# Attention of block 1 with transposed scores, and an earlier start of its output product

## The chip, the cores and the metric

One core of one Trainium2 chip runs the whole program in one launch. The metric is the device time in microseconds (us), median of the runs shown. The engines are called by what they do: TensorE (PE in the profile) multiplies matrices, PEld is its load of the stationary side; VectorE is DVE, ScalarE is ACT, GpSimd is POOL, SyncE is SP, from which most DMAs are issued.

## The reference

512 tokens of width 1024 pass twice through block 1 (a mixer of attention and a two-way state-space scan, then a feed-forward part) and once through block 2. The change is in block 1's mixer alone:

```python
    def one_block(qi):
        s = jnp.einsum("bqgrd,bkgd->bgrqk", qi, k)
        p = jax.nn.softmax(s, axis=-1)
        return jnp.einsum("bgrqk,bkgd->bqgrd", p, v)
...
        attn_out = blocked_gqa(q, k, v).astype(x.dtype)
        ssd_out = ssd_mixer(z, xbc_raw, dt_raw, conv_w[i], conv_b[i], dt_bias[i], a_log[i],
                            d_skip[i], ssd_norm_w[i])
        mixed = jnp.concatenate([attn_out, ssd_out], axis=-1)
        x = x + jnp.einsum("ble,ed->bld", mixed, w_out[i])
```

There are 8 query heads of 64 and 2 key/value heads, over 512 tokens; the state-space part has 8 heads, 4 chunks of 128 tokens and both directions.

## The kernel before

All data are fp32. Large products are made of three fp32r products of split operands: each factor is held as a high part (rounded to fp32r) and a low part (the rest), and high x high, high x low and low x high are summed in PSUM. One such product of a 128 x 128 weight tile with 512 tokens is a "row": the three passes of lines 1469 to 1471. The weights are streamed from HBM in slots, and each slot is split by ScalarE (high, L1805) and VectorE (low, L2216). Small products are in plain fp32, which the trace shows as two passes for each product; a transpose is one pass.

The instructions of every engine stand in one fixed order. The class Order writes it down beforehand by playing the program through with a table of costs (TIMES, in us) and a few delays (DELAY). Each chain of work (attention, conv, ssd_decay, ssd_rows, ...) is a generator that adds its steps when their inputs are due by that clock and when PSUM banks are free (room, take, free). Every engine then runs its part of that order strictly in sequence, with semaphores where data cross. There are eight PSUM banks; while the input projection runs, three serve its rows and five ("side") all the rest; afterwards all eight serve both.

Block 1 of layer l: the wide product gives z, v and dt with tokens on partitions; thirteen column tiles follow (k, four of q, eight of x, B and C for the convolution). After each q or k tile come its norm, rotation and split (rsq, rmm, rroot, rcs, rope, qhi, qlo; SP swaps halves by DMA into ROT). Then come attention and the state-space part, then the output product.

Attention before, for each pair of heads and block of 128 queries (16 such steps, pair_chunk, and two head_chunk each):

- qk (L1686, L1687): scores with queries on partitions and 512 keys along the row, from the high and low keys; each head's high and low queries lie in the two halves of 128 partitions.
- max, exp with the sum as a second output, nrm (reciprocal), prs (scaling), on VectorE and ScalarE (L2494, L2000, L2499, L2006).
- pT (L1428): four 128 x 128 transposes for each head, and pta (L2013), their copy.
- pv (L1701): eight products for the two heads, in two column halves of the array.
- yv (L2018 on ScalarE, L2504 on VectorE): the split of 128 tokens of output into YHI and YLO.

State space, for each chunk c of four: dec (L1645, products of 32 rows in four row groups, into four banks), dexp (ScalarE), mask, w and xc (VectorE), off and yt (PE), goff, ytc, yb (transposes), gyb, gsq and zout (L2479); after the last chunk four transposes of Z (zT, L1428) and yz. The output product of layer l is split: the first four output tiles are made as one group, row after row, r = 0 to 3 being attention's and 4 to 7 the state-space part's; the other four follow. It begins when all outputs of attention and the last yb have been put into the order:

```python
        self.run(lambda: ("yv", l, NH // 2 * CH - 1) in self.n and ("yb", l, CH - 1) in self.n)
```

X waits in HBM meanwhile and is brought back by GpSimd's DMAs after the last yz.

## Time and profile before

| what | value |
|---|---|
| median of 3 runs | 2699.52 us (2699.2 to 2699.63) |
| the profiled execution: span | 2697.8 us, 1.7 us under the median; the rest lies before and after its first and last instruction |
| TensorE, VectorE, ScalarE busy in the span | 99%, 57%, 43% |
| granted TensorE clock | 0.999 of 2.4 GHz |
| block 1, layer 0: projection ends, output product begins | 127.6 us, 206.3 us |
| layer 1: the same | 734.2 us, 812.8 us |

A row of the profile gives busy time or a start and a duration. TensorE's durations include the time in which a pass drains, which overlaps the next one; what a pass costs in a flow is the distance between starts. Times are from the start of the span.

### The profile page before, as it was taken

The page shows a single profiled execution, that of the slowest core. Times are in us where ns is not written, and L with a number is a line of the kernel's source. Part 1 is how long each engine was busy: PE and PEld are TensorE (multiplying, and loading weights), DVE is VectorE, ACT ScalarE, POOL GpSimd, SP SyncE. Part 2 cuts the span into 40 slices and gives each one's busy share as a digit, 9 for nine tenths or more (in the row PEclk, how much of TensorE's full clock was granted, in tenths as well). Part 3 has the DMA queues.
Part 4 walks back from the last instruction along what each step waited for, and adds up shares of the span by engine and source line. Part 5 has one row for each costly group of instructions (what it writes and reads, how often), then busy time and mean ns, then how long its engine had stood idle before and what let it go on. Part 6 is the DMA issues. An engine that isn't in the chain of part 4 may idle for free.

```text
span 2697.8 us, 33846 instructions
## 1 busy us (share of the span) xinstructions
PE 2665.9 (99%) x13860; PEld 2195.1 (81%) x13860; DVE 1526.9 (57%) x2142; ACT 1173.5 (43%) x1732; POOL 26.8 (1%) x45
## 2 busy tenths in 40 slices
PE   9989999999989999999999999999999999999998
PEld 8777888888777888888888888888777888888887
DVE  7885444345885444344444356899978844544433
ACT  6784332225784322233322234455688452432221
POOL 0000000000000000000000000000000000000000
PEclk9999999999999999999999999999999999999999
DMA  6303333324303333333333342222223432333332
GB/s 216 94 2 110 100 96 95 98 83 148 94 2 110 102 94 97 97 94 97 100 94 96 98 138 86 72 74 76 77 86 96 133 94 94 98 98 94 98 94 67
DMA packets 75801, 255.55 MB, mean 95 GB/s; under 512 B 9088, under 2 KB 12288, under 8 KB 75264
## 3 DMA queue, kind: packets, MB, share of 16 engines
q1 hardware_dynamic: 73136, 240.29, 29.3%
q0 software_dynamic: 2512, 13.11, 1.3%
q8 instruction: 110, 1.80, 0.3%
q14 instruction: 43, 0.35, 0.0%
HBM read 241.30 MB, written 8.39 MB: 93 GB/s over the span
## 4 chain that ended last, share of the span: by engine, by line
PE 93%; DVE 4%; ACT 3%; issue 1%; DVEq 0%; ACTq 0%
PE PS L1469 27%; PE PS L1471 27%; PE PS L1470 27%; PE PS L1719 1%; PE PS L1701 1%; PE PS L1428 1%; PE PS L1488 1%; PE PS L1487 1%; PE PS L1489 1%; DVE WLO L2216 0%; PE PS L1665 0%; ACT WHI L1805 0%; PE PS L1537 0%; PE PS L1535 0%; PE PS L1539 0%
## 5 line engine op out<-in xcount | busy, mean ns | idle before, releaser
L1469 PE MATMUL PS<-HHI,WHI 128*128 128x512 f32 x2256 | 893.2, 396 | 0.0
L1471 PE MATMUL PS<-HHI,WLO 128*128 128x512 f32 x2256 | 878.8, 390 | 0.0
L1470 PE MATMUL PS<-HLO,WHI 128*128 128x512 f32 x2256 | 878.3, 389 | 0.0
L2216 DVE TENSOR_TENSOR WLO<-WR,WHI 128x1024 fp32r<-128x1024 f32 (+2 forms) x450 | 535.0, 1191 | 495.4 <-ACT WHI L1805 492.2
L1805 ACT CAST WHI<-WR 128x1024 fp32r<-128x1024 f32 (+2 forms) x450 | 457.5, 1018 | 445.6 <-PE PS L1471 421.9
L1469 PEld LDWEIGHTS PS<-HHI,WHI 128*128 128x128 f32 x2256 | 423.6, 188 | 92.1 <-issue 4.8
L1470 PEld LDWEIGHTS PS<-HLO,WHI 128*128 128x128 f32 x2256 | 423.7, 188 | 89.9 <-issue 4.1
L1471 PEld LDWEIGHTS PS<-HHI,WLO 128*128 128x128 f32 x2256 | 423.4, 188 | 88.8
L1469 PE MATMUL PS<-FHI,WHI 128*128 128x512 f32 x682 | 265.3, 389 | 0.0
L1470 PE MATMUL PS<-FLO,WHI 128*128 128x512 f32 x682 | 265.3, 389 | 0.0
L1471 PE MATMUL PS<-FHI,WLO 128*128 128x512 f32 x682 | 265.3, 389 | 0.0
L1877 ACT CAST FHI<-SQF 128x512 fp32r<-128x512 f32 x88 | 54.5, 620 | 330.3 <-DVE SQF L2285 330.3
L1873 ACT ACTIVATE SQF<-SQF 128x512 f32<-128x512 f32 x88 | 55.6, 632 | 307.4 <-DVE SQF L2278 307.3
L2606 DVE SCALAR_TENSOR_TENSOR CVA<-CU,VEC,CVA 128x511 f32<-128x511 f32 (+14 forms) x240 | 162.9, 730 | 1.8 <-ACT CVA L2110 1.8
L2285 DVE TENSOR_TENSOR SQF<-SQF,PS 128x512 f32<-128x512 f32 x88 | 60.6, 688 | 166.0 <-PE PS L1471 162.1
L1469 PEld LDWEIGHTS PS<-FHI,WHI 128*128 128x128 f32 x682 | 128.0, 188 | 26.8
L1470 PEld LDWEIGHTS PS<-FLO,WHI 128*128 128x128 f32 x682 | 128.0, 188 | 26.5
L1471 PEld LDWEIGHTS PS<-FHI,WLO 128*128 128x128 f32 x682 | 128.0, 188 | 26.4
L2278 DVE TENSOR_TENSOR SQF<-PS,RS 128x512 f32<-128x512 f32 x88 | 60.8, 691 | 142.2 <-PE PS L1471 140.9
L1469 PE MATMUL PS<-YHI,WHI 128*128 128x512 f32 x320 | 128.1, 400 | 2.2 <-DVE WLO L2216 2.1
L1471 PE MATMUL PS<-YHI,WLO 128*128 128x512 f32 x320 | 124.7, 390 | 0.0
L1470 PE MATMUL PS<-YLO,WHI 128*128 128x512 f32 x320 | 124.6, 389 | 0.0
(381 smaller groups left out, 2727.5 us busy)
## 6 DMA issues: line engine op xcount, KB each, us to landing
WR<-in_stream SPq DMA_DIRECT2D x402, 512.0 KB, 3.6
WR<-in_stream SPq DMA_DIRECT2D x32, 384.0 KB, 3.0
xkeep<-X POOLq DMA_DIRECT2D x3, 2048.0 KB, 9.4
X<-xkeep POOLq DMA_DIRECT2D x24, 256.0 KB, 4.7
WR<-in_stream SPq DMA_DIRECT2D x16, 328.0 KB, 4.0
ROT<-RQ SPq DMA_DIRECT2D x40, 64.0 KB, 2.0
X<-in_xin SPq DMA_DIRECT2D x8, 256.0 KB, 4.9
out<-X SPq DMA_DIRECT2D x8, 256.0 KB, 2.2
```

What stands on the lines that cost most here:

```text
L1428: t = e.transpose(out[:, i * P:(i + 1) * P], src, ident)
L1469: e.matmul(out, hi[:, i, :], xhi, start=first, stop=False)
L1470: e.matmul(out, hi[:, i, :], xlo, start=False, stop=False)
L1471: t = e.matmul(out, lo[:, i, :], xhi, start=False, stop=final)
L1487: e.matmul(out, xhi, hi[:, i, :], start=r == 0, stop=False)
L1805: e.copy(hi, raw).then_inc(S["act_high"], 1)
L1873: e.activation(SQ[:, j % 2, :], SQ[:, j % 2, :], ACT.Silu).then_inc(S["act_silu"], 1)
L1877: e.copy(FHI[:, j, :], HF[:, j % 2, :]).then_inc(S["act_xhigh"], 1)
L2216: e.tensor_tensor(lo, raw, hi.bitcast(F32), ALU.subtract).then_inc(S["dve_low"], 1)
L2278: e.tensor_tensor(SQ[:, j % 2, :], PS[o.bank["gate", f, j]][:, :], RS[:, :], ALU.mult).then_inc(S["dve_gs"], 1)
L2285: e.tensor_tensor(HF[:, j % 2, :], SQ[:, j % 2, :], PS[o.bank["up", f, j]][:, :], ALU.mult).then_inc(S["dve_mul"], 1)
L2606: e.scalar_tensor_tensor(acc[:, s:T], CU[:, j, 0:T - s], vec("cvw", 8 * (TAPS - 1 - s) + j), acc[:, s:T], ALU.mult, ALU.add).then_inc(S["d ...
```

## The change

The scores are computed twice. First qk makes them as before with queries on partitions, but from high parts alone, with 64 rows for each of two heads, and only for the maximum of each query (over tokens c, c + 4, c + 8, ... for each c of four). The negated maxima of a head (NM) go by DMA (mrow) as one row under a copy of the head's high queries (qdup, also a DMA) in QM. Then ks makes the scores with keys on partitions: the high keys times the queries' high and low parts, plus the low keys and a row of ones times QM, so that the maximum is already subtracted. exp of that needs no sum and no scaling, and its result is the stationary side of pv, which moves V with a column of ones (65 columns) and gives for each head tokens on partitions with the sum in column 64. yn divides by it; after two heads hT transposes four 128 x 128 blocks and yv splits 512 tokens at once. Exponentials lie in five buffers, and in nine after the 24th tile. The transposes of probabilities, their copies, the scaling and the accumulated sums are gone. GpSimd sets the ones by two memsets. The delays pace1 and pace2 become 0.1. The output product's group is put into the order once yt of chunk 2 is, and each attention row needs only its own pair of heads. The core of the diff (the semaphore names, group names and times of removed steps are left out, and in the functions of the class Order the removed lines too):

```diff
-    "qk": (("pe", 0.92),), "qhi": (("act", 0.76785),), "qlo": (("dve", 1.3),), "pT": (("pe", 0.45),), "pv": (("pe", 0.95),),
+    "qk": (("pe", 0.25),), "ks": (("pe", 0.46),), "mrow": (("sp", 0.3),), "qdup": (("sp", 0.1),), "qhi": (("act", 0.76785),), "qlo": (("dve", 1.3),), "hT": (("pe", 0.45),), "pv": (("pe", 1.9),),
...
-DELAY = {"v": 0.38043, "zsilu": 0.77358, "pace1": 0.37491, "pace2": 6.0781, "turned": 0.81963, "sums": 0.30369, "ss": 1.401,
-         "hsum": 0.075925, "picked": 0.55886, "lru": 5.6906, "sq": 0.27228, "third": 0.17664, "merged": 0.20081, "until": 0.087442}
+DELAY = {"v": 0.38043, "zsilu": 0.77358, "pace1": 0.1, "pace2": 0.1, "turned": 0.81963, "sums": 0.30369, "ss": 1.401,
+         "hsum": 0.075925, "picked": 0.55886, "lru": 5.6906, "sq": 0.27228, "third": 0.17664, "merged": 0.20081, "until": 0.087442, "row": 2.6}
...
-PR_OF = [i % 3 if i < 8 else (3, 4, 2, 0, 1)[(i - 8) % 5] for i in range(4 * NH)]
-PR_BEFORE = {i: max(k for k in range(i) if PR_OF[k] == PR_OF[i]) for i in range(4 * NH) if PR_OF[i] in PR_OF[:i]}
+TILES = NH * CH
+EARLY = 24
+PT_OF = [i % 5 if i < EARLY else (4, 5, 6, 7, 8, 0, 1, 2)[i - EARLY] for i in range(TILES)]
+PT_BEFORE = {i: max(k for k in range(i) if PT_OF[k] == PT_OF[i]) for i in range(TILES) if PT_OF[i] in PT_OF[:i]}
...
+    def maxima(self, l, m):
+        for c in range(CH):
+            yield from self.room(2)
+            while self.tokens_wait:
+                yield 0.1
+            for h in (2 * m, 2 * m + 1):
+                self.take(("qk", l, h, c), "side")
+            yield self.add("qk", l, m, c)
+            for h in (2 * m, 2 * m + 1):
+                last = self.add("max", l, h, c)
+                self.free(("qk", l, h, c), ("dve_max", last))
+            yield self.pace
+        yield last
+        for h in (2 * m, 2 * m + 1):
+            self.spawn(self.head(l, h))
+    def head(self, l, h):
+        if h > 0:
+            yield from self.added(("ks", l, h - 1, CH - 1))
+        if h >= 2:
+            yield from self.until(("ks", l, h - 2, CH - 1))
+        self.add("qdup", l, h)
+        self.add("mrow", l, h)
+        yield DELAY["row"]
+        for k in range(CH):
+            i = CH * h + k
+            if i in PT_BEFORE:
+                yield from self.added(("pv", l, PT_BEFORE[i] // CH))
+            if PT_OF[i] >= 5:
+                yield from self.added(("qlo", l, 4))
+            yield from self.room()
+            while self.tokens_wait:
+                yield 0.1
+            self.take(("ks", l, h, k), "side")
+            yield self.add("ks", l, h, k)
+            exp = self.add("exp", l, i)
+            self.free(("ks", l, h, k), ("act_exp", exp))
+            yield self.pace
         yield exp
+        if h > 0:
+            yield from self.added(("yn", l, h - 1))
         yield from self.room()
+        self.take(("pv", l, h), "side")
+        yield self.add("pv", l, h)
+        done = self.add("yn", l, h)
+        self.free(("pv", l, h), ("dve_yn", done))
+        if h % 2:
+            yield done
+            yield from self.room()
+            self.take(("hT", l, h // 2), "side")
+            yield self.add("hT", l, h // 2)
+            self.free(("hT", l, h // 2), ("dve_yv", self.add("yv", l, h // 2)))
 
     def attention(self, l):
         yield from self.until(("v", l))
+        for m in range(NH // 2):
+            yield from self.until(("kdup", l), ("qlo", l, 1 + m))
+            if m > 0:
+                yield from self.added(("qk", l, m - 1, CH - 1))
+            self.spawn(self.maxima(l, m))
 
...
-        self.run(lambda: ("yv", l, NH // 2 * CH - 1) in self.n and ("yb", l, CH - 1) in self.n)
+        self.run(lambda: ("yt", l, 2) in self.n)
         self.advance(SPL)
         self.product_group(("mixed", l), [(("out", 2 * l, j), "w_out", l, j * P) for j in range(CH)],
-                           {DT - 4 + i: ("yz", l, i) for i in range(4)})
+                           {i: ("yv", l, i) if i < 4 else ("yz", l, i - 4) for i in range(DT)})
...
-    V = sb("V", 192, [CH, P])
-    PR = sb("PR", 194, [2, T])
-    PT = sb("PT", 198, [2, 2, CH, P])
-    NM = sb("NM", 206, [8])
-    RSM = sb("RSM", 206.0625, [8])
-    RIN = sb("RIN", 206.125, [8])
+    V = sb("V", 192, [CH, 2, 65])
+    PT = sb("PT", 194.03125, [5, T])
+    QM = (sb("QM", 76, [T], F32R), sb("QM2", 204.03125, [T], F32R))
+    NM = sb("NM", 206.03125, [NH, CH], F32R)
+    RIN = sb("RIN", 206.1875, [2, CH])
+    YVS = (sb("YV", 180, [4, T]), sb("YV2", 207.5, [4, T]))
...
-                        q.wait_ge(S["dve_yv"], n["yv", of[0], CH * r + CH - 1])
+                        q.wait_ge(S["dve_yv"], n["yv", of[0], r])
...
             elif kind == "qk":
-                l, u = a
-                m, c = u // CH, u % CH
-                q.wait_ge(s_keys, 64 * (l + 1))
+                l, m, c = a
+                q.wait_ge(s_keys, 48 * (l + 1))
                 q.wait_ge(S["dve_qlow"], n["qlo", l, 1 + m])
-                for i in range(2):
-                    emptied(q, ("qk", l, 2 * u + i))
-                    out, left = PS[o.bank["qk", l, 2 * u + i]][:, :], query(2 * m + i)[:, c * P:(c + 1) * P]
-                    e.matmul(out, left, KDS[0][:, m // 2, :], start=True, stop=False)
-                    t = e.matmul(out, left, KDS[1][:, m // 2, :], start=False, stop=True)
+                for i, half in enumerate((slice(0, 64), slice(64, P))):
+                    emptied(q, ("qk", l, 2 * m + i, c))
+                    t = e.matmul(PS[o.bank["qk", l, 2 * m + i, c]][:, :], query(2 * m + i)[half, c::CH],
+                                 KDS[0][half, m // 2, :], start=True, stop=True)
                 t.then_inc(S["pe_qk"], 1)
-            elif kind == "pT":
-                l, i = a
-                q.wait_ge(S["act_prs"], n["prs", l, i])
-                transposes(step, [PRS[PR_OF[i]][:, k * P:(k + 1) * P] for k in range(CH)]).then_inc(S["pe_turn"], 1)
+            elif kind == "ks":
+                l, h, k = a
+                emptied(q, step)
+                q.wait_ge(S["pool_ones"], 2 * l + 2)
+                q.wait_ge(s_qm[h % 2], 32 * (4 * l + h // 2 + 1))
+                keys = slice(k * P, (k + 1) * P)
+                e.matmul(PS[o.bank[step]][:, :], KDS[0][:, h // 4, keys], query(h), start=True, stop=False)
+                e.matmul(PS[o.bank[step]][:, :], KDS[1][0:65, h // 4, keys], QM[h % 2][0:65, :], start=False, stop=True
+                         ).then_inc(S["pe_ks"], 1)
             elif kind == "pv":
-                l, u = a
-                m = u // CH
+                l, h = a
+                out = PS[o.bank[step]]
                 emptied(q, step)
+                q.wait_ge(S["pool_ones"], 2 * l + 1)
                 q.wait_ge(S["act_v"], n["v", l])
-                q.wait_ge(S["act_pt"], n["pta", l, 2 * u + 1])
-                for k in range(CH):
-                    for i in range(2):
-                        t = e.matmul(PS[o.bank[step]][64 * i:64 * i + 64, 0:P], V[:, k, 64 * (m // 2):64 * (m // 2) + 64],
-                                     PT[:, u % 2, i, k, :], start=k == 0, stop=k == CH - 1)
+                q.wait_ge(S["act_exp"], n["exp", l, CH * h + CH - 1])
+                for c in range(CH):
+                    for k in range(CH):
+                        t = e.matmul(out[:, 65 * c:65 * c + 65], PTS[PT_OF[CH * h + k]][:, c * P:(c + 1) * P], V[:, k, h // 4, :],
+                                     start=k == 0, stop=k == CH - 1)
                 t.then_inc(S["pe_pv"], 1)
+            elif kind == "hT":
+                l, m = a
+                emptied(q, step)
+                q.wait_ge(S["dve_yn"], n["yn", l, 2 * m + 1])
+                transposes(step, [heads_tokens(m)[:, c, :] for c in range(CH)]).then_inc(S["pe_turn"], 1)
...
             elif kind == "exp":
                 l, i = a
-                k = i % 8
-                q.wait_ge(S["dve_max"], n["max", l, i])
-                if i in PR_BEFORE:
-                    q.wait_ge(S["pe_turn"], n["pT", l, PR_BEFORE[i]])
-                elif i >= 8:
-                    q.wait_ge(S["dve_qlow"], n["qlo", l, 2])
-                e.activation(PRS[PR_OF[i]], PS[o.bank["qk", l, i]][:, :], ACT.Exp, bias=NM[:, k:k + 1],
-                             accum_out=RSM[:, k:k + 1]).then_inc(S["act_exp"], 1)
-            elif kind == "prs":
-                l, i = a
-                k = i % 8
-                q.wait_ge(S["dve_nrm"], n["nrm", l, i // 2])
-                e.activation(PRS[PR_OF[i]], PRS[PR_OF[i]], ACT.Copy, scale=RIN[:, k:k + 1]).then_inc(S["act_prs"], 1)
-            elif kind == "pta":
-                l, i = a
-                u = i // 2
-                q.wait_ge(S["pe_turn"], n["pT", l, i])
-                if u >= 2:
-                    q.wait_ge(S["pe_pv"], n["pv", l, u - 2])
-                e.copy(PT[:, u % 2, i % 2, :, :].rearrange("p k q -> p (k q)"), PS[o.bank["pT", l, i]][:, :]).then_inc(S["act_pt"], 1)
+                q.wait_ge(S["pe_ks"], n["ks", l, i // CH, i % CH])
+                if PT_OF[i] >= 5:
+                    q.wait_ge(S["dve_qlow"], n["qlo", l, 4])
+                if i in PT_BEFORE:
+                    q.wait_ge(S["pe_pv"], n["pv", l, PT_BEFORE[i] // CH])
+                e.activation(PTS[PT_OF[i]], PS[o.bank["ks", l, i // CH, i % CH]][:, :], ACT.Exp).then_inc(S["act_exp"], 1)
             elif kind == "yv":
-                l, u = a
-                at_ = slice(u % CH * P, (u % CH + 1) * P)
-                q.wait_ge(S["pe_pv"], n["pv", l, u])
-                e.copy(YHI[:, u // CH, at_], PS[o.bank["pv", l, u]][:, 0:P]).then_inc(S["act_yv"], 1)
+                l, m = a
+                q.wait_ge(S["pe_turn"], n["hT", l, m])
+                e.copy(YHI[:, m, :], PS[o.bank["hT", l, m]][:, :]).then_inc(S["act_yv"], 1)
...
             elif kind == "max":
-                l, i = a
-                k = i % 8
-                q.wait_ge(S["pe_qk"], n["qk", l, i // 2])
-                if i >= 8:
-                    q.wait_ge(S["act_exp"], n["exp", l, i - 8])
-                e.tensor_reduce(NM[:, k:k + 1], PS[o.bank["qk", l, i]][:, :], AX, ALU.max, negate=True).then_inc(S["dve_max"], 1)
-            elif kind == "nrm":
-                l, u = a
-                k = 2 * u % 8
-                q.wait_ge(S["act_exp"], n["exp", l, 2 * u + 1])
-                e.reciprocal(RIN[:, k:k + 2], RSM[:, k:k + 2]).then_inc(S["dve_nrm"], 1)
+                l, h, c = a
+                q.wait_ge(S["pe_qk"], n["qk", l, h // 2, c])
+                e.tensor_reduce(NM[:, h, c:c + 1], PS[o.bank["qk", l, h, c]][:, :], AX, ALU.max, negate=True).then_inc(S["dve_max"], 1)
+            elif kind == "yn":
+                l, h = a
+                got = PS[o.bank["pv", l, h]][:, 0:65 * CH].rearrange("p (c x) -> p c x", c=CH)
+                q.wait_ge(S["pe_pv"], n["pv", l, h])
+                settle(e.reciprocal(RIN[:, h % 2, :], got[:, :, 64]))
+                e.tensor_tensor(heads_tokens(h // 2)[:, :, 64 * (h % 2):64 * (h % 2) + 64], got[:, :, 0:64],
+                                RIN[:, h % 2, :].unsqueeze(2).to_broadcast([P, CH, 64]), ALU.mult).then_inc(S["dve_yn"], 1)
             elif kind == "yv":
-                l, u = a
-                at_ = slice(u % CH * P, (u % CH + 1) * P)
-                q.wait_ge(S["act_yv"], n["yv", l, u])
-                e.tensor_tensor(YLO[:, u // CH, at_], PS[o.bank["pv", l, u]][:, 0:P], YHI[:, u // CH, at_].bitcast(F32),
+                l, m = a
+                q.wait_ge(S["act_yv"], n["yv", l, m])
+                e.tensor_tensor(YLO[:, m, :], PS[o.bank["hT", l, m]][:, :], YHI[:, m, :].bitcast(F32),
                                 ALU.subtract).then_inc(S["dve_yv"], 1)
...
+            elif kind == "v":
+                l, = a
+                done(q, ("z", l))
+                e.memset(V[:, :, :, 64:65], 1.0).then_inc(S["pool_ones"], 1)
+            elif kind == "kdup":
+                l, = a
+                q.wait_ge(s_keys, 48 * (l + 1))
+                q.wait_ge(S["pool_ones"], 2 * l + 1)
+                e.memset(KDS[1][64:65, :, :].bitcast(F32), 1.0).then_inc(S["pool_ones"], 1)
...
+            elif kind == "qdup":
+                l, h = a
+                rows = slice(0, 64) if h % 2 == 0 else slice(64, P)
+                q.wait_ge(S["act_qhigh"], n["qhi", l, 1 + h // 2])
+                if h >= 2:
+                    q.wait_ge(S["pe_ks"], n["ks", l, h - 2, CH - 1])
+                elif l > 0:
+                    q.wait_ge(S["dve_xlow"], n["hlo", 2 * l, DT - 1])
+                e.dma_start(QM[h % 2][0:64, :].bitcast(F32), query(h)[rows, :].bitcast(F32)).then_inc(s_qm[h % 2], 16)
+            elif kind == "mrow":
+                l, h = a
+                q.wait_ge(S["dve_max"], n["max", l, h, CH - 1])
+                e.dma_start(QM[h % 2][64:65, :].bitcast(F32), NM[:, h, :].bitcast(F32)).then_inc(s_qm[h % 2], 16)
             elif kind == "vectors":
```

## Rows read from the trace of the kernel before

**Rows 1.** The page, busy time of each engine over the span.
```profile
PE 2665.9 (99%) x13860; PEld 2195.1 (81%) x13860; DVE 1526.9 (57%) x2142; ACT 1173.5 (43%) x1732; POOL 26.8 (1%) x45
```
**Rows 2.** Windows: length, busy PE, PEld, DVE, ACT, POOL (instructions), clock, DMA, GB/s.
```profile
80.00:127.60 47.60, 47.56 (x245) 37.73 (x244) 37.15 (x57) 36.67 (x66) 0.54 (x1) 1.00 0.31 97
127.60:206.30 78.70, 69.66 (x838) 56.40 (x836) 66.79 (x132) 69.11 (x163) 4.66 (x4) 1.00 0.01 2
206.30:220.00 13.70, 13.05 (x66) 10.55 (x65) 6.36 (x10) 5.03 (x11) 2.12 (x4) 1.00 0.20 51
734.20:812.80 78.60, 69.58 (x836) 56.33 (x835) 66.75 (x132) 69.02 (x163) 4.66 (x4) 1.00 0.01 2
```
**Rows 3.** Timeline of PE, 118 to 124 us: start, duration, instruction.
```profile
119.36 0.40 PE L1471 MATMUL PS<-HHI,WLO 128*128 128x512 f32 x1
119.80 0.63 PE L1428 MATMUL PS<-CON,PR 128*128 128x128 f32 x4
120.18 0.47 PE L1469 MATMUL PS<-HHI,WHI 128*128 128x512 f32 x1
120.49 0.39 PE L1470 MATMUL PS<-HLO,WHI 128*128 128x512 f32 x1
120.72 0.40 PE L1471 MATMUL PS<-HHI,WLO 128*128 128x512 f32 x1
```
**Rows 4.** Waits, 127.6 to 206.3 us: who for whom, total, times, longest.
```profile
DVE YLO L2504 <- ACT YHI L2018: 7.8, 5, 3.6
...
PE PS L1428 <- DVE YLO L2504: 1.9, 2, 1.7
...
PE PS L1428 <- ACT PR L2000: 1.4, 1, 1.4
...
PE PS L1624 <- ACT PR L2000: 0.6, 1, 0.6
...
PE PS L1428 <- ACT PT L2013: 0.5, 1, 0.5
```
**Rows 5.** Timeline of PE, 151.45 to 157.9 us.
```profile
152.53 1.97 PE L1701 MATMUL PS<-PT,V 128*64 128x128 f32 x32
154.42 1.17 PE L1645 MATMUL PS<-RUNB,RUNA 32*128 32x128 f32 x32
155.53 0.50 PE L1686 MATMUL PS<-KDH,QS 128*128 128x512 f32 x1
```
**Rows 6.** PE's groups, 127.6 to 206.3 us: busy us, mean ns, idle before.
```profile
L1701 PE MATMUL PS<-PT,V 128*64 128x128 f32 x224 | 14.6, 276 | 1.2 <-DVE RUNB L2432 0.8 <-ACT PT L2013 0.4
```
**Rows 7.** Timeline of PE, 55.25 to 56.9 us: the cumulative sums.
```profile
55.53 1.22 PE L1607 MATMUL PS<-SD,CON 128*128 128x64 f32 x10
56.56 0.48 PE L1469 MATMUL PS<-HHI,WHI 128*128 128x512 f32 x1
```
**Rows 8.** ScalarE's groups, 127.6 to 206.3 us.
```profile
L2013 ACT COPY PT<-PS 128x512 f32<-128x512 f32 x28 | 15.5, 608 | 0.8 <-PE PS L1428 0.6
...
L2006 ACT ACTIVATE PR<-PR,RIN 128x512 f32<-128x512 f32 x11 | 7.7, 751 | 0.0
```
**Rows 9.** VectorE's groups, 127.6 to 206.3 us.
```profile
L2494 DVE TENSOR_REDUCE NM<-PS 128x1 f32<-128x512 f32 x24 | 15.4, 683 | 1.6 <-PE PS L1687 1.6
...
L2504 DVE TENSOR_TENSOR YLO<-PS,YHI 128x128 fp32r<-128x128 f32 x14 | 4.0, 287 | 8.0 <-ACT YHI L2018 7.8
...
L2499 DVE RECIPROCAL RIN<-RSM 128x2 f32<-128x2 f32 x13 | 1.9, 156 | 0.0
...
L2442 DVE TENSOR_TENSOR MF<-PS,CON 128x256 f32<-128x256 f32 x4 | 1.7, 417 | 0.0
```
**Rows 10.** DMA issues: out, engine, count, KB each, median us to landing.
```profile
ROT<-RQ SPq DMA_DIRECT2D x40, 64.0 KB, 2.0
...
KDH<-KDH SPq DMA_DIRECT2D x4, 128.0 KB, 4.3
```
**Rows 11.** Timeline, 209 to 236 us: VectorE's last scaling and the first transpose.
```profile
209.50 0.61 DVE L2479 TENSOR_SCALAR Z<-YA,SS 128x256 f32<-128x256 f32 x2 [0.40 <-ACT SS L1788]
...
212.09 0.60 PE L1428 MATMUL PS<-CON,Z 128*128 128x128 f32 x4
```

77 lines of the change are left out of this document (17 added, 60 removed).

## The prediction

> **What bounds the kernel now.** I began with the page's busy shares: TensorE is in use for 99% of the span [rows 1]. A busy row of TensorE includes its drain, so this says that little is idle, not that nothing can be saved. Next came the windows view, cut where block 1 changes character [rows 2]. While the input projection runs (80 to 127.6 us) TensorE is busy to within 0.04 us. From the projection's last product (127.6) to the first of the output product (206.3) there is a stretch of 78.7 us with attention and the state-space part alone. There TensorE is busy 69.66 us, ScalarE 69.11, VectorE 66.79: three engines, each close to full and each waiting for the others. The second layer has the same stretch from 734.2, of 78.6 us. The reader is to see that only these two stretches hold idle time, 9.0 us each by this view. Outside them TensorE has none, so that each product added there is paid in full, and attention that is moved ahead of 127.6 only changes sides.
>
> More than 9.0 us is slack, since drains hide in busy. The timeline shows the edges [rows 3]: starts of rows follow each other in about 0.23 us, but with four transposes between them, 119.36 to 120.49 holds two rows and the burst: 1.13 us, less 0.46 is 0.67, where four transposes in steady flow take 0.44 (priced below). So a burst of plain fp32 that stands alone costs 0.23 us of edges besides its work. The waits of the stretch [rows 4] name who is late: TensorE waits 4.4 us for scaled probabilities, copies of transposes and exponentials on ScalarE, or for VectorE at YLO; VectorE itself stood 7.8 us behind ScalarE's copy of an attention output. ScalarE's queue is the place where attention and state space get into each other's way.
>
> **Products of one layer.** Scores before: 16 steps of four 512-wide fp32r passes; passes of this width stand 0.23 apart [rows 3]: 64 x 0.231 = 14.8 us. After: the transposed scores (ks) are 32 steps of two such passes, again 14.8; the maxima's pass (qk) is 16 steps of two products of 64 rows each, in the two halves of the array. The only row-tiled products here are the decay's, 32 rows high: 32 passes in 155.53 - 154.42 = 1.11 us [rows 5], 0.035 each, where a full pass takes 0.11 (below). So row tiles run side by side; I take 0.25 for a pair, 4.0 us, and 0.46 (one after the other), 7.4, as the other end. The decay's burst has an edge of its own: eight groups of four at 0.11 are 0.88, and it took 1.11. Sixteen such edges would be 3.7 us; I put 1 against what is given back below.
>
> The Trainium skill ("TensorEngine Tiling (Array Packing)", section Key Properties) has every change of the tiling mode drain TensorE. That speaks against many single pairs among full products; at the decay's edge, by estimate, it would make the sum 2.7 us a layer worse than mine.
>
> Transposes before: 32 x 4 = 128; after: 16. The burst of four in [rows 3] gives 0.095 (0.38 / 4, its end hidden by the next product) to 0.117 (0.63, less 0.28 for one, over three steps); at 0.109 each this is -112 x 0.109 = -12.2 us.
>
> Output of attention (pv) before: 16 steps of 16 passes in column halves; two steps took 154.42 - 152.53 = 1.89 us [rows 5], so 0.95 a step and 15.2 us. After: 8 steps of 16 products, fp32, thus two passes each, with probabilities of 128 x 128 as the stationary side and 65 columns moving. The nearest row is the cumulative sum: a 128 x 128 stationary side, 64 columns moving, ten passes in 1.22 us by the row, less the 0.27 to 0.28 that one fp32 pass lasts [rows 6], over nine steps: 0.105; from its start to the next product 1.03, 0.103 [rows 7]. I take 0.11, as these passes are no faster than transposes that move 128 columns: the stationary side sets the pace. 8 x 32 x 0.11 = 28.2 us, +13.0. The lower bound is the pace of the old column halves, 1.89 / 32 = 0.059: 15.1 us, so 0.
>
> The Trainium skill ("TensorE: Matmul & The Clock Gate", section LDWEIGHTS) has the load of a stationary side take its columns over 1.2 GHz whatever the rows, 107 ns for 128; the trace agrees with 0.103 to 0.105. The same page's isolated gap ("Back-to-back issue gap") would make a 65-column pass about 30 ns, a step of 32 under 1 us and the layer's pv 7.6 us, an estimate that the row of the cumulative sum speaks against.
>
> Sum on TensorE: +4.0 - 12.2 + 13.0 = **+4.8 us a layer**, +8.2 with the pairs in series.
>
> **The other engines, a layer.** ScalarE loses 32 rescalings of 0.75 and 32 copies of 0.61 [rows 8] (in steady flow some 0.1 less each), its 32 reads of the accumulator and twelve of sixteen output copies: about 40 us of work, some 33 of it in the stretch, where it was 69 of 78.7. VectorE keeps 32 maxima of 0.68; the small outputs (16 of 0.29) and reciprocals give way to 8 divisions over 256 columns, priced at 0.42 as the mask of that width out of PSUM plus a reciprocal, and 4 outputs of 512, 0.69: 4.6 + 2.4 out, 4.6 + 2.8 in [rows 9]. That is nothing, but VectorE keeps its 67 us in the stretch, and 206.3 can come no nearer than that to 127.6.
>
> Five tiles hold a head's exponentials until the seventh head, so three of four exponentials wait for the pv of the head before; that pv stands ahead of their scores in TensorE's order, so this adds nothing by itself, but it lets no head run ahead of its neighbour.
>
> New on SP's queue: eight copies of the query's high half and eight rows of maxima. The SBUF copies of before land 2.0 us (64 KB) to 4.3 us (128 KB) after issue [rows 10]. TensorE has 49.2 / 8 = 6.2 us of work a head and there are two buffers, so I cost them at nothing; without that cover (the first head, and any whose maxima are late) it is 2 to 4.3 us each. In the projection these DMAs wait between the weight loads, and a load behind them has the 5.5 us that 24 rows give it. On GpSimd two small memsets stand before the limits' DMA: nothing, as its queue is empty. VectorE's division waits for the whole pv of 3.5 us, with maxima and state-space work queued behind; that is the wait that takes YLO's place.
>
> **What is given back, a layer.** (1) Of the 4.4 us of TensorE's waits in [rows 4] I count 3.5 as gone: the instructions at fault are removed or ScalarE is half empty. (2) Edges: 48 fp32 bursts of attention become 12, at most 36 x 0.23 = 8.3 us less. Many stand beside other fp32 work and share edges, and 14 of the 16 old pv are in the stretch [rows 6], so I take 4, less the 1 of the pairs: 3. (3) The output product starts with the attention rows of four tiles, 48 passes or 11 us, while the last chunks run; before, it began at 206.3, when VectorE's last scaling stood at 209.50 and the first transpose of it at 212.09 [rows 11]. The moved passes are no less work; what they fill is idle time, 0.65 us of the third window of [rows 2] and, as an estimate, 1.9 of the 9.0 of the second, at its end: 2.5. Sum 9.0. Against +4.8: **-4.2 a layer, -8.4 in all**. The profiled execution's span is 2697.8 us; its time is 1.7 less than the median 2699.5, so the median becomes about **2691**. Both ends for the range: everything given back (9.0 + 0.65 + 8.3 = 18.0) is -13.2 a layer, 2673; nothing, and pairs in series, +8.2, 2716.
>
> **Rivals.** *The added passes win* (slower). Place: the stretch. If the divisions behind pv and the maxima behind the score banks bring back as much waiting as ScalarE's relief removes, only the sum of products is left: +4.8 x 2 = +9.6, 2709, with pairs in series 2716. For it: VectorE has 67 us in the stretch, and the order's cost table calls pv 1.9 where I get 3.5, so eight times 1.6 us are scheduled as if free. Against it: TensorE is then the one that is never idle. It decides from less than 4.8 us a layer given back. Chance 0.23.
>
> *Even.* The output product holds four of the eight banks, and the last chunk's decay wants four at once; it then comes after all attention, the 2.5 us of (3) are lost, and one or two late rows of maxima take another 2: -4.2 + 4.5, 2700, range 2695 to 2704. Chance 0.17.
>
> *Most is given back.* With ScalarE out of the way the order packs TensorE nearly full: 14 us instead of 9.0, -9.2 a layer, 2681. The same time would come if the 65-column passes were at the lower bound (13.0 less a layer would even give 2665); of this end a tenth of this case. Chance 0.13.
>
> My forecast has 0.47, its own range 2685 to 2695.
>
> **How the numbers follow.** Under 2694.1 (0.2%, about what a measurement of this kernel can tell from no change) lie the whole of the third rival and nearly all of the forecast, 0.44: faster 0.57. Within it: 0.17 and 0.03: same 0.20. Slower 0.23. The range runs from 2676 to 2710: below it lies half of the third rival's tail, above it the pairs in series.
>
> **What the profile would show.** The pv line with 512 passes in two layers, 3.4 to 3.6 us a step of 32, and qk's two passes starting within some ns; if they are 0.23 apart, the maxima cost double. Between the projection's last product and the last transpose of the state-space output, ScalarE down from 69 to about 35 to 40 us busy, VectorE still at 65 to 70, TensorE's idle time under 5 us. Rows of the output product between the last two chunks. Wrong I would be if ks waited for SP's DMAs in most heads, if VectorE stood for whole pv steps while a decay burst waited for its banks, or if the old idle time of 9.0 us was there under new names.

## The result and the profile after

The change made the kernel slower: median 2724.51 us (2721.7 to 2727.13, 4 runs) against 2699.47, ratio 1.0091, 95% interval [1.0077, 1.0105]. I had forecast 2691 with a range up to 2710 and given "slower" 0.23. The profiled execution's span is 2722.9 us, 25.1 above that of before. Where the first layer's mixer is done (the sum of the next norm) is at 264.52 us before and 274.94 after, in layer 1 at 871.09 and 894.48: +10.4 and another +13.0, so all but 1.7 us of the loss is where the change is. The last 1.7 us are the spell of half clock at 2084 us that comes up below, in block 2, where both kernels do the same work. Of the experiments' executions, two stand at a far lower granted clock (11248.86 us at 0.226 with the wide pv, 4646.68 us at 0.623 with GpSimd's queue and full maxima) and are in no comparison.

The page after, and the windows view (columns as in [rows 2]), cut at the projection's end, the first output row, and the same in layer 1:

```profile
PE 2690.1 (99%) x13700; PEld 2216.7 (81%) x13700; DVE 1530.4 (56%) x2118; ACT 1086.4 (40%) x1512; POOL 27.8 (1%) x49
```
```profile
80.00:143.30 63.30, 58.81 (x284) 46.29 (x282) 47.17 (x71) 27.72 (x45) 0.54 (x1) 0.97 0.27 74
143.30:204.10 60.80, 58.59 (x631) 49.38 (x630) 50.56 (x91) 30.01 (x60) 3.09 (x3) 0.97 0.06 13
204.10:232.00 27.90, 24.64 (x160) 20.24 (x159) 12.83 (x24) 8.16 (x22) 1.04 (x1) 1.00 0.06 20
700.00:763.00 63.00, 58.11 (x277) 45.79 (x275) 45.55 (x70) 26.66 (x44) 0.59 (x2) 0.95 0.26 74
```

Against [rows 2] two things are new. The stretch without projection and output rows shrank from 78.7 us with 9.0 idle to 60.8 with 2.2 idle, as hoped; but the projection, in which TensorE had not been idle at all, now ends 15.7 us later (part of that is attention moved ahead) and holds 4.5 us of idle time. And the granted clock, 1.00 in every window of before, is 0.97 in the projection and in the stretch of layer 0, and 0.95 in the projection of layer 1.

The timeline at the idle time, SP's queue and TensorE together (start, duration; SPq is the issue of a DMA):

```profile
103.02 0.51 SPq L2765 DMA_DIRECT2D ROT<-RQ  x1
103.57 0.59 SPq L2766 DMA_DIRECT2D ROT<-RQ  x1
104.20 0.59 SPq L2765 DMA_DIRECT2D ROT<-RQ  x1
104.27 0.39 PE L1485 MATMUL PS<-HHI,WLO 128*128 128x512 f32 x1
104.83 0.59 SPq L2766 DMA_DIRECT2D ROT<-RQ  x1
105.47 0.59 SPq L2781 DMA_DIRECT2D QM<-QS  x1
106.11 0.59 SPq L2785 DMA_DIRECT2D QM<-NM  x1
108.28 0.77 PE L1707 MATMUL PS<-QS,KDH 128*128 128x512 f32 x1 [3.63 <-DMA QM<-NM]
```
VectorE in the same trace, its last maxima for the first two heads:
```profile
93.82 1.29 DVE L2500 TENSOR_REDUCE NM<-PS 128x1 fp32r<-128x512 f32 x2 [0.85 <-PE PS L1698]
```

The maxima were done at 95.1, and their row was issued at 106.11, 11.0 us later. It stood on SP behind the copies of the next query tile (ROT<-RQ), which had to wait for ScalarE to evict that tile. TensorE is then idle for 3.63 us (4.01 between starts, where a pass takes 0.23). The second head's row costs 0.87 us of idle time, about 1.2 between starts beyond the pass; in layer 1 it is 4.04 and 0.84. These four are all the waits of ks for its DMAs: in each layer the other six heads don't wait.

TensorE's rows for the new products:

```profile
131.18 0.39 PE L1707 MATMUL PS<-QS,KDH 128*128 128x512 f32 x1
131.41 0.40 PE L1708 MATMUL PS<-QM,KDL 65*128 65x512 f32 x1
131.74 0.63 PE L1698 MATMUL PS<-KDH,QS 64*128 64x512 f32 x2
132.30 0.50 PE L1483 MATMUL PS<-HHI,WHI 128*128 128x512 f32 x1
132.63 0.40 PE L1484 MATMUL PS<-HLO,WHI 128*128 128x512 f32 x1
...
136.87 3.68 PE L1719 MATMUL PS<-V,PT 128*128 128x65 f32 x32
140.49 0.62 PE L1698 MATMUL PS<-KDH,QS 64*128 64x512 f32 x2
```

ks is 0.23 a pass; pv is 140.49 - 136.87 = 3.62 us for 32 passes, 0.11 each. The maxima's pair (its two passes start 3 to 4 ns apart in 30 of the trace's 32 pairs, at most 9, so they run side by side) takes 0.56 us from its start to the next row's, and the full passes ahead of it and behind it take 0.33 instead of 0.23: 0.76 us in all for 0.23 of work, 0.53 of edges. Behind a pv burst, which has its own edge, the pair adds less.

The granted clock in its spells, by windows cut to them:

```profile
107.90:111.30 3.40, 3.02 (x7) 2.47 (x8) 3.07 (x7) 1.71 (x3) 0.00 (x0) 0.50 0.25 49
148.80:152.20 3.40, 3.40 (x49) 2.24 (x51) 3.40 (x7) 0.56 (x1) 0.00 (x0) 0.51 0.21 40
725.70:732.50 6.80, 6.22 (x13) 4.29 (x14) 4.90 (x9) 2.31 (x4) 0.00 (x0) 0.50 0.25 77
```

0.50 is 1.2 of 2.4 GHz. The clock of the first and third falls in or behind the idle 3.63 and 4.04 us, that of the second behind 1.98 us in which TensorE waits for VectorE's convolution (2.6 between starts). With two more (766.6, 3.4 us; 2084.2, 3.4 us) these are 20.4 us at half speed. TensorE is idle for 1.1 of them, so some 9.7 us are lost, an estimate. Before has no such spell until its last 4.2 us.

A gap of this size does not always bring a spell. The last of the five stands behind a gap in block 2 that before has too, and there the clock stays:

```profile
2060.46 1.12 PE L1766 MATMUL PS<-XB,GW 128*128 128x512 f32 x2 [1.89 <-DVE XB L2613]
```
```profile
2055.00:2075.00 20.00, 18.11 (x76) 14.01 (x75) 18.15 (x24) 17.96 (x22) 0.00 (x0) 1.00 0.37 112
```
and in the trace after:
```profile
2083.84 1.76 PE L1789 MATMUL PS<-XB,GW 128*128 128x512 f32 x2 [1.87 <-DVE XB L2620]
```
```profile
2084.20:2087.60 3.40, 3.40 (x6) 1.42 (x5) 3.33 (x5) 3.37 (x4) 0.00 (x0) 0.50 0.47 137
```

So spells come and go between executions, and a difference between two kernels has to be freed of them. The table takes from each profiled execution's span half of the time at half clock in which TensorE was not idle (the last microseconds of the program left out). The last column is thus an estimate of the span at full clock.

| kernel | span, us | half clock, us | span at full clock, estimate |
|---|---|---|---|
| before | 2697.8 | 0 | 2697.8 |
| changed | 2722.9 | 20.4 | 2713.2 |
| early start alone | 2713.5 | 13.6 | 2707.7 |
| early start after the last decay | 2700.5 | 0 | 2700.5 |
| late start | 2719.9 | 17.1 | 2711.6 |
| full maxima | 2717.5 | 13.6 | 2711.6 |
| each pair twice | 2726.1 | 13.7 | 2720.2 |
| scores due later | 2737.1 | 68.3 | 2703.4 |
| GpSimd's queue | 2708.9 | 10.2 | 2703.9 |
| wide pv | 2731.8 | 30.7 | 2717.5 |
| wide pv, full maxima, late start | 2711.7 | 13.6 | 2705.0 |
| full maxima, late start, price altered | 2719.9 | 27.3 | 2708.6 |
| the same on GpSimd's queue | 2718.6 | 20.5 | 2709.5 |
| no maxima | 2697.6 | 10.2 | 2692.5 |
| GpSimd's queue, full maxima | 2705.7 | 10.2 | 2700.8 |
| GpSimd's queue, full maxima, late start | 2701.2 | 6.8 | 2698.0 |

### The profile page after: what moved, and what is told of

It reads as the page before. It is cut to its first block, busy times and chain, and to the rows that moved or that the text cites. A ratio compares the mean times of both kernels' runs of the same rounds, so it can differ in the third digit from the quotient of the medians.

```text
span 2722.9 us, 33265 instructions
## 1 busy us (share of the span) xinstructions
PE 2690.1 (99%) x13700; PEld 2216.7 (81%) x13700; DVE 1530.4 (56%) x2118; ACT 1086.4 (40%) x1512; POOL 27.8 (1%) x49
## 4 chain that ended last, share of the span: by engine, by line
PE 93%; DVE 4%; ACT 2%; issue 1%; SPq 0%; DMA 0%; DVEq 0%; ACTq 0%
PE PS L1483 27%; PE PS L1485 27%; PE PS L1484 27%; PE PS L1719 2%; PE PS L1742 1%; PE PS L1502 1%; PE PS L1503 1%; PE PS L1501 1%; PE PS L1707 1%; DVE WLO L2225 0%; PE PS L1789 0%; PE PS L1708 0%; PE PS L1551 0%; PE PS L1549 0%; PE PS L1698 0%
## 5 line engine op out<-in xcount | busy, mean ns | idle before, releaser
L2287 DVE TENSOR_TENSOR SQF<-PS,RS 128x512 f32<-128x512 f32 x88 | 60.8, 691 | 141.6 <-PE PS L1485 140.3
```

Source lines behind the costliest of these rows:

```text
L2287: e.tensor_tensor(SQ[:, j % 2, :], PS[o.bank["gate", f, j]][:, :], RS[:, :], ALU.mult).then_inc(S["dve_gs"], 1)
```

## The experiments

Each time is a median. Before was run beside each group of them on the same chip (2699.75 to 2700.84); the groups ran on different chips, so a difference between kernels of two groups is uncertain by about 1 us. The table above names them all.

**The early start by itself**, in the kernel before:

```diff
-        self.run(lambda: ("yv", l, NH // 2 * CH - 1) in self.n and ("yb", l, CH - 1) in self.n)
+        self.run(lambda: ("yt", l, 2) in self.n)
...
-                           {DT - 4 + i: ("yz", l, i) for i in range(4)})
+                           {i: ("yv", l, CH * i + CH - 1) if i < 4 else ("yz", l, i - 4) for i in range(DT)})
```


> The kernel before with the second part of the change alone: the output product of four tiles is put into the order once the third state-space product is, attention as it was. Theory A (the time went to the attention part: its products, the edges of the score pairs, the late row of maxima with the clock behind it): no loss, 0 to -5 us against before, since the stretch has idle time that the moved rows fill. Theory B (four banks held while the last chunks run starve the decays): slower by 5 us or more, 2705 or above.

Measured 2715.70, ratio 1.0059 [1.0044, 1.0074]: theory B's time. The last decay burst, before and here, and what comes of it:

```profile
195.94 1.17 PE L1645 MATMUL PS<-RUNB,RUNA 32*128 32x128 f32 x32
```
```profile
207.47 1.17 PE L1645 MATMUL PS<-RUNB,RUNA 32*128 32x128 f32 x32
...
221.64 1.71 PE L1428 MATMUL PS<-CON,Z 128*128 128x128 f32 x8 [3.73 <-DVE Z L2479]
```

The decay moved by 11.5 us, the whole chain of the last chunk behind it, and TensorE ran out of rows: 3.73 us idle, then 6.8 us of half clock.

**The same, but gated by the last decay**:

```diff
-        self.run(lambda: ("yt", l, 2) in self.n)
+        self.run(lambda: ("dec", l, CH - 1) in self.n)
```


> The kernel before with the early output product alone, but its group of four banks is put into the order only after the last chunk's decay (which itself wants four banks) has been. Theory A (the 16 us lost by the early start alone came from the last decay, which had to wait for the group's banks): 2694 to 2701, the last decay back at about 196 us and no gap of 4 us before the transposes of Z. Theory B (the group's banks starve the rest of the chunk, or its rows simply stand in front of it, whatever the decay does): 2704 or more, with the last scaling of Z later than the 209.50 us of before.

Measured 2703.84, 1.0014 [1.0005, 1.0023]; the decay is at 195.68 again. The loss against before fell from 15.9 to 3.0 us, so 13 us hang on the last decay, some 6 of them through half clock (6.8 us in each layer of the first trace, none in this one). That it waited for banks, and not behind the rows, follows from the order's code, not from a run: a chain that is due is put in after at most one row, and played through by its own clock the order asks for the decay's four banks at 187.8 in both kernels and gets them at 203.2 before, at 214.5 with the early start. The other 3 us are a cost of the moved rows that no run splits. The start gains nothing in either case; the time lies between the ranges of the two theories.

**The changed kernel without the early start** (the old condition in terms of its own steps):

> The changed kernel with the output product put into the order as late as before. Theory A: the same or slower than the changed kernel, 2723 to 2734, as the 11 us of rows no longer fill the last chunks. Theory B (the early start costs more than it fills): 2703 to 2715.

Measured 2722.29 (before 2699.76): 2.2 us gained, under the range of A and above that of B; at full clock it is 1.6 by the table. In the changed kernel the last decay (193.85) happens to be ahead of the group, so that its banks cost nothing here.

**Maxima from full products** (the other half of the 128 rows is the keys' copy times the queries' low part, as before):

```diff
-                    t = e.matmul(PS[o.bank["qk", l, 2 * m + i, c]][:, :], query(2 * m + i)[half, c::CH],
-                                 KDS[0][half, m // 2, :], start=True, stop=True)
+                    t = e.matmul(PS[o.bank["qk", l, 2 * m + i, c]][:, :], query(2 * m + i)[:, c::CH],
+                                 KDS[0][:, m // 2, :], start=True, stop=True)
```


> The changed kernel, but the pass for the maxima is made of full products of 128 rows (high and low query against the high key) in place of pairs of 64 rows side by side; nothing else. If the pair is dear because of its edges (0.55 us in the trace for 0.23 of work), two full products at 0.46 without edges are cheaper: 16 x 0.09 = 1.4 us a layer, and 2 to 6 us in all with what the edges cost their neighbours, 2718 to 2722. If the pairs are worth their edges in the stretch, where they stand two by two, it is slower: up to 16 x 0.2 x 2 = 7 us, 2731.

Measured 2720.48, the first case: twice the work of the concurrent pairs, and yet 4.0 us less. Not all of it is the pairs' edges: the profiled execution has 13.6 us of half clock instead of 20.4, and at full clock the gain is 1.6 by the table. In the trace a full pair among rows takes 0.46 to 0.47 and its neighbours their 0.23.

**Each pair twice**:

> The changed kernel with each of the maxima's pairs of 64-row products issued twice in a row (each of the 32 score blocks of a layer is computed twice; the output is unchanged). Theory A (a pair costs an edge, the change of the array's mode, and little work): the second pair shares the edge and adds one concurrent pair, 0.23 us: 16 x 0.23 = 3.7 us a layer, 7.4 in all, 2729 to 2735 beside 2724.5; in the trace a step of two pairs lasts about 0.8 us among full rows where one pair costs 0.55. Theory B (the pairs run one after the other, 0.46 of work a pair): +7.4 a layer, 2737 to 2742. Theory C (every pair pays the 0.55 anew): +8.8 a layer, 2740 to 2745.

Measured 2727.89, +3.4. A step of two pairs:

```profile
134.47 0.87 PE L1699 MATMUL PS<-KDH,QS 64*128 64x512 f32 x4
135.27 0.50 PE L1483 MATMUL PS<-HHI,WHI 128*128 128x512 f32 x1
```

0.80 where one pair takes 0.56: the second costs its 0.24, the edge is paid once. B and C are out by the time and by the trace. The +3.4 seems less than half of A's 7.4, but this trace has 13.7 us of half clock instead of 20.4; at full clock the difference is +7.0 by the table, which is A's. The clock hid half of the work.

**The first heads' scores due later**, in the order alone:

```diff
-        yield DELAY["row"]
+        yield DELAY["row"] + (4.0 if h == 0 else 1.5 if h == 1 else 0.0)
```


> The changed kernel with its order planned for a later row of maxima: the first head's scores are due 6.6 us after the row is sent instead of 2.6, the second's 4.1. No instruction changes, only the order. Theory A: the idle 3.6 and 4.0 us in the projection, the 0.9 us of the second head and most of the half-clock behind them go: -8 to -14 us, 2711 to 2717. Rival (the wait only moves to the next step, for attention has no slack): within 3 us of the changed kernel.

Measured 2738.84, 2711.96, 2723.77 and 2737.78 (median 2730.78), with granted clocks of 0.987, 0.998, 0.993 and 0.987. The gaps are gone, and the run that kept its clock is where theory A had it; the median is not. The profiled one lost it for 30.7 us in each layer (window, then the timeline's pv bursts inside it and after it):

```profile
148.80:179.50 30.70, 30.67 (x137) 24.22 (x136) 12.24 (x22) 7.72 (x14) 0.00 (x0) 0.50 0.07 14
```
```profile
150.47 7.06 PE L1719 MATMUL PS<-V,PT 128*128 128x65 f32 x32
164.13 7.09 PE L1719 MATMUL PS<-V,PT 128*128 128x65 f32 x32
178.53 3.74 PE L1719 MATMUL PS<-V,PT 128*128 128x65 f32 x28
```

TensorE is busy throughout this stretch and still stays at 1.2 GHz; nothing like it is in the trace of before. Nor is there a gap to blame: from 80 us to the fall at 148.8 the longest is this one.

```profile
146.72 0.50 PE L1707 MATMUL PS<-QS,KDH 128*128 128x512 f32 x1 [0.70 <-DVE RUNB L2441]
```

So the half clock behind the gaps may go with the gaps in one execution and come back without any in the next; why it fell here is open. At full clock this kernel is at 2703.4 by the table, as GpSimd's queue is below (2703.9): both repairs of the late row are worth the same.

**The two small DMAs on GpSimd's queue**, nothing else (the qdup and mrow branches are moved from SP's program to GpSimd's):

> The changed kernel with the two small DMAs of each head (the copy of the queries and the row of maxima) issued from GpSimd's queue instead of SP's; order and all else as they are. Theory A (the gaps of 4.0 and 4.4 us before the first head's ks arise because the row stands behind four ROT copies of 0.6 us on SP): the row is issued some 2.4 us earlier, the gap shrinks to about 1.6 us, and with one spell of half clock a layer less: 2714 to 2720. Theory B (the row is late because the maxima are late and the landing takes 2.3 us, whichever queue issues it): the gaps stay over 3 us and the time 2722 to 2727.

Measured 2709.01, 1.0035 [1.0022, 1.0048]: 15.5 us less than the changed kernel (16.4 if each is taken against before on its own chip), more than any theory. GpSimd's queue, then the first head's ks and the projection's window:

```profile
95.34 0.57 POOL L2740 DMA_DIRECT2D QM<-NM  x1 [20.04 <-DVE NM L2500]
95.91 0.53 POOL L2736 DMA_DIRECT2D QM<-QS  x1
96.43 0.57 POOL L2740 DMA_DIRECT2D QM<-NM  x1
```
```profile
105.03 0.39 PE L1707 MATMUL PS<-QS,KDH 128*128 128x512 f32 x1
```
```profile
80.00:137.50 57.50, 57.50 (x287) 45.87 (x287) 47.59 (x72) 28.25 (x46) 2.73 (x5) 1.00 0.29 84
```

Both rows are issued by 97.0 instead of 106.7 and later; TensorE is never idle in this projection again and its clock is 1.00. I had counted only the four copies of 0.6 us in front of the row, not the wait of the first of them. The sum closes within a microsecond or two: four gaps less one pass each are 3.8 + 1.2 + 4.2 + 1.2 = 10.4 us, and half clock fell from 20.4 to 10.2 us, some 4.8 us of time, together 15.2; the two profiled executions are 14.0 apart, the medians 15.5.

**pv turned round** (V with 64 columns of ones stationary, 512 queries moving; no hT; ScalarE makes the reciprocal of the sums):

```diff
-                for c in range(CH):
-                    for k in range(CH):
-                        t = e.matmul(out[:, 65 * c:65 * c + 65], PTS[PT_OF[CH * h + k]][:, c * P:(c + 1) * P], V[:, k, h // 4, :],
-                                     start=k == 0, stop=k == CH - 1)
+                for k in range(CH):
+                    t = e.matmul(out[:, :], V[:, k, h // 4, :], PTS[PT_OF[CH * h + k]], start=k == 0, stop=k == CH - 1)
```


> The changed kernel with pv turned round: V with 64 columns of ones beside it is the stationary side (128 x 128), and the exponentials of 512 queries move, so a head is 4 products, 8 passes of 512 columns, instead of 16 products of 65 columns. Outputs come out with features on partitions, so the four transposes for two heads (hT) go; ScalarE makes the reciprocal of the sums (Ln, then Exp of the negative), VectorE multiplies. Theory A (what slows the changed kernel is the 3.5 us a head of narrow passes, and the clock that falls in the stretch where they stand): 8 passes of 0.21 to 0.23 are 1.7 to 1.85 us a head, 1.7 less, 13.6 a layer, and hT's 0.44 x 4 = 1.8 less: up to -15 a layer, -30 in all; with half of it lost to VectorE's and ScalarE's added work on the way (some 0.7 and 1.3 us a head more) 2695 to 2712, and no half clock between 145 and 200 us. Theory B (the bound of the stretch is not TensorE's work but VectorE and the waits): 2718 to 2728.

Measured 2733.1, above both ranges. The premise was wrong:

```profile
122.14 3.59 PE L1717 MATMUL PS<-PT,V 128*128 128x512 f32 x8
```

The next product starts 3.03 us after this burst and takes 0.40 more than usual, so a plain fp32 pass of 512 columns costs 0.43 us, and a head is 3.4 to 3.6 us both ways round. What was added is ScalarE's and VectorE's work, and the clock fell all the same: 30.7 us of half clock in this trace. **With full maxima and the late start**:

> The kernel of the last one, also with the maxima from full 128-row products (no change of the array's mode) and the output product put into the order as late as before. Theory A: another 1.4 us a layer for the products of the maxima and about 1 a layer for the start (as measured for each alone: 4.0 and 2.2 in all): 2689 to 2706, which is at or under the kernel before (2699.5). Theory B: with the stretch bound by VectorE both are worth nothing here: within 3 us of the wide pv alone.

Measured 2714.61, 18.5 less than the wide pv alone. Both theories missed: in this order the rows of maxima of the first two heads were issued at 97.54 and 104.37, where nothing waited for them. **The narrow pv with the same two parts undone** (and, as in the kernel just shown, the price of qk in the table set to 0.46):

> The changed kernel with two parts undone: the maxima from full 128-row products (issued with their true price in the order's cost table) and the output product put into the order as late as before. Theory A (the two costs are separate and add): 2724.5 - 4.0 - 2.2, 2716 to 2720. Theory B (what counts is how the order falls, since both shift it): as in the kernel with the wide pv, whose order had no wait for a row of maxima at all, 2705 to 2714. Beside that kernel it also prices the wide pv's extra VectorE and ScalarE work: TensorE's work is the same in both within 2 us a layer.

Measured 2721.38, above both ranges, though no ks waits for a row of maxima here either. The new order placed the last chunk's products badly:

```profile
210.23 0.69 PE L1679 MATMUL PS<-DE,XCF 128*64 128x128 f32 x4 [4.91 <-DVE XCB L2458]
```

and 10.2 us of half clock follow. **With GpSimd's queue too**:

> The changed kernel with full-width maxima, the late output product, and the small DMAs on GpSimd's queue together. Theory A (separate costs that add): 2708 to 2715. Theory B (the queue brings nothing beyond the other two): the same as those two alone, within 2 us. If transposed scores could be had without loss, this should come within 0.2% of the kernel before (2705); I expect it does not, since the +4.8 us of products a layer remain.

Measured 2720.79, theory B: the queue brings nothing where the order has already moved the rows out of harm, and the same idle 4.91 us stand in it. A changed price in the order's table is thus a change of its own, worth more than the part under test.

**Without the maxima's pass** (it leaves out qk, the maxima, their rows and their waits, and so the softmax's maximum):

```diff
-                e.activation(PTS[PT_OF[i]], PS[o.bank["ks", l, i // CH, i % CH]][:, :], ACT.Exp).then_inc(S["act_exp"], 1)
+                e.activation(PTS[PT_OF[i]], PS[o.bank["ks", l, i // CH, i % CH]][:, :], ACT.Exp, scale=1.0 / 64).then_inc(S["act_exp"], 1)
```


> The changed kernel without the pass for the maxima: no qk, no maxima, no copies of queries and rows by DMA; the scores are not shifted and exp takes 1/64 of them, so this leaves out the softmax's maximum and changes its scale. ks is still two full passes a tile. Theory A (the pass costs its products at the measured 0.55 us a pair, 8.8 us a layer, and the waits for its rows of maxima, 5.5 to 5.8 us a layer in the changed kernel): 2 x 14.4 less, 2692 to 2699. Theory B (products alone, the waits' room being filled by others): 2705 to 2709. Theory C (VectorE's 22 us of maxima a layer were the bound of the stretch): under 2690.

Measured 2700.32, 1.0001 [0.9992, 1.0011]: the pass with all that hangs on it costs 24.2 us in the changed kernel, and the rest of the change, transposed scores with their pv, is as fast as the old attention. A missed by 1.3 us; B and C are out. The order changed with the pass: it has idle times of its own, 2.9 us ahead of 191.4 and 2.3 for a late weight tile ahead of 199.5, and 10.2 us of half clock.

**The cost table left alone**, so that TensorE's order stays the changed kernel's: GpSimd's queue with full maxima, and then with the late start too.

> The changed kernel with the small DMAs on GpSimd's queue and the maxima from full 128-row products; the order of steps is that of the changed kernel on TensorE, VectorE and ScalarE. Theory A (the edge of each pair of 64-row products is a cost of its own on TensorE): 16 pairs a layer at 0.55 become two passes at 0.23 each, 1.4 us a layer less than the 2709.0 of the queue alone, 2705 to 2707. Theory B (the 4 us that the full products brought in the changed kernel were its spells of half clock, of which it had two fewer): no gain beside the queue, 2708 to 2710.

> The same, with the output product put into the order as late as before as well, but with the cost table left as in the change, so that the order of the attention stays that of the changed kernel. Theory A (the three costs add when the order is not disturbed; the 2720.8 of the kernel with all three was its order, where a product of the state-space output waited 5.2 us for VectorE): 2701 to 2705. Theory B (the late start is needed less now or costs its own gap): 2706 to 2710. In either case not below 2697.

Measured 2706.7, 1.0024 [1.0014, 1.0033], and 2703.01, 1.0012 [1.0004, 1.0021]. Theory A in both: now the parts add, -15.5, -2.3, -3.7 (-16.4, -1.7 and -3.7, each taken against before on its own chip). Both kernels with GpSimd's queue have 10.2 us of half clock, so the -2.3 is not the clock's. Where the last comes from shows in the first transposes of Z and the row after them (timeline, early start, then late):

```profile
216.76 0.50 PE L1483 MATMUL PS<-YHI,WHI 128*128 128x512 f32 x1 [0.81 <-DVE YLO L2511]
...
219.62 1.03 PE L1442 MATMUL PS<-CON,Z 128*128 128x128 f32 x8
221.78 0.50 PE L1483 MATMUL PS<-YHI,WHI 128*128 128x512 f32 x1 [1.13 <-DVE YLO L2494]
```
```profile
211.40 0.60 PE L1442 MATMUL PS<-CON,Z 128*128 128x128 f32 x4
211.75 0.48 PE L1483 MATMUL PS<-YHI,WHI 128*128 128x512 f32 x1
```

Late, attention rows stand between the four bursts and cover the way over ScalarE and VectorE; early, they have been used up. These two waits are 1.9 us a layer in the first trace; the second has one of 0.7 us there (for YT), so 1.2 us a layer are gained. The two profiled executions are 4.5 us apart; 1.7 of that is a spell at 2068 in block 2 that only the first has. The last kernel is the best found, and still 3.3 us behind the kernel before; its eleven runs lie between 2700.55 and 2706.45, those with a granted clock of 0.999 at 2700.55 to 2702.59 and those with 0.997 at 2704.92 to 2706.45. At full clock it is level with before by the table (2698.0 and 2697.8): what is left is clock.

## Why the prediction was wrong, point by point

- **The step "so I cost them at nothing", for the copies and rows of maxima on SP's queue, failed, and it was the largest.** I bounded the row's landing (2 to 4.3 us; 2.0 measured from issue) and not when SP would come to issue it. The text named the case ("without that cover ... 2 to 4.3 us each") and gave SP's queue one sentence, about loads behind the new DMAs and not about what stands ahead of them. The ROT copies wait for a projection tile, so the row waited 11.0 us in a queue. Price: 15.5 us of the 25, by the run that changed the queue alone. The sign I had named, ks waiting in most heads, would not have shown it: two heads of eight wait, and they are enough.
- **The clock was not a term at all.** It is some 9.7 us of the 25.1 between the two profiled executions, 4.8 of them inside the 15.5. [Rows 2] have 1.00 throughout, and I took it as fixed. With the idle 1.98 us for the convolution, which the reordering brought, spells stay even where the queue is mended.
- **"I take 0.25 for a pair" with an edge of at most 0.23 was too low.** The passes run side by side as said, but a pair among rows costs 0.76, and less beside other bursts. Full products, 7.4 us a layer, are 2.3 us faster in all in the kernels with equal clock, so the pairs' own price is about 8.6 a layer where I had 4.0 and an edge allowance of 1 (at full clock by the table the gain is 1.6 to 3.1, the price 8.2 to 9.0). The Trainium skill's rule ("TensorEngine Tiling (Array Packing)", Key Properties) that a change of the mode drains TensorE agrees; its estimate in the prediction (2.7 a layer worse) was nearer than my sum, and still about 1 us a layer too low.
- **Term (3), the early output product at -2.5 a layer, had the wrong sign.** It costs 3.7 us in all in the mended kernel, 2.2 in the changed one. I counted the idle time that the rows would fill and not the idle time that they had been filling, behind the transposes of Z. The 0.65 us of the third window was besides a wait for a weight tile (WLO, at 209.25), which no moved row can fill. The rival *Even* had the mechanism of the four banks: it is real (the early start alone loses 16 us, 13 of them with the late decay), but not at work in the changed kernel.
- **pv at 0.11 a pass, 3.5 us a step, was right** (3.49 to 3.72 from its start to the next product), and so was ScalarE's relief (30.0 us busy in the stretch). That VectorE would keep its 67 us there was not: it has 50.6, since part of its work moved into the projection (47.2 us busy there, 37.2 before), and so the stretch could become 17.9 us shorter.
- **Terms (1) and (2), waits and edges given back, were right in size once the new wait is gone.** The last kernel has no pairs, so there they are 3.5 and 4, 7.5 us a layer. It adds 8.2 us of products a layer by the prediction's prices (4.8, and 3.4 for full products of the maxima) and its span is 3.4 us longer in all, so that 16.4 less 3.4, 6.5 us a layer, came back, and with its half clock taken off 8.1 (an estimate). No run splits waits from edges. In the changed kernel, with 4.8 a layer added and 25.1 us lost, nothing came back.
- **Of the rivals**, *The added passes win* has the sign, but its place (the stretch, VectorE) and its 2709 are wrong: the loss is in the projection. 2724.5 lay outside the range since no case held a DMA that is late by its queue.

The ledger over both layers, from 2699.5: my forecast for the products and terms (1) and (2), without the 1 us for edges of the pairs and without (3), is 2 x (4.8 - 7.5) = -5.4; the pairs at 8.6 a layer instead of 4.0, +9.2; the early start +3.7; the row's lateness with its clock +15.5: 2722.5. The remaining 2.0 us is not resolved; the spell in block 2, 1.7 us, may be among them.

The same by the table, between profiled executions: of the 25.1 us, 9.3 are the late row at full clock, 3.1 the pairs beyond full products, 2.8 the early start, 0.2 all the rest of the change with full products for the maxima in it, and 9.7 half clock.

## What to carry to other kernels

Cost a small DMA by when its queue comes to it: list what stands ahead of it in program order and what each of those waits for, and give it a queue whose earlier entries don't wait (11 us late on SP, at once on GpSimd). Before explaining a difference of a few microseconds, count the time at half clock in both traces: here it made +7.0 us of added work look like +3.4. Before moving work earlier to fill a hole, ask which hole it fills where it stands now. And when an order is planned by a cost table, change one thing with the table held fixed: the same three repairs gave 2720.8 with one price altered and 2703.0 without (at full clock 2709.5 and 2698.0, by the same estimate).

## What the hardware showed that was not expected

- A pair of 64-row products in the two halves of the array costs 0.53 us of edges when it stands alone among full products (0.10 ahead, 0.33 within, 0.10 behind); two pairs in a row pay them once (0.80 within for four passes).
- A plain fp32 pass moves 512 columns in 0.43 us and 65 columns in 0.11, where an fp32r pass of 512 takes 0.23: for narrow ones the stationary side sets the pace ("TensorE: Matmul & The Clock Gate" of the Trainium skill, section LDWEIGHTS, has the load take its columns over 1.2 GHz, 107 ns for 128 by estimate, and the 0.11 of the trace agrees), for wide ones the columns.
- The granted clock fell to 1.2 GHz behind idle times of 1.9 to 4.0 us in the changed kernel, and not behind the one of 1.9 us in the kernel before. In the kernel with the scores due later it fell with no idle time over 0.7 us ahead of it and stayed down for 30.7 us in which TensorE was busy for 30.67; the four runs of that kernel have clocks of 0.987 to 0.998. What in that stretch takes it down and keeps it there was not tried.
